# Four edits in a two-block transformer kernel: gate rows under the root, an earlier exponential, output banks closed one by one, and a last norm on two engines

## The chip, the core and the metric

The kernel runs on one core of a Trainium2 chip, alone. The metric is the device time of one execution in microseconds (us), the median of three runs. In the profile the engines are PE (matrix products), PEld (its weight loads), DVE (vector), ACT (scalar), POOL and SP; SP issues nearly all DMAs here. PE has two clock levels, 1.2 and 2.4 GHz; the profile's granted clock is 0.5 at the lower and 1.0 at the higher one.

## What is computed

256 tokens of width 1024 pass through two blocks. The first has two layers (feed-forward, attention, feed-forward, with layer norms). The second has two layers on the same rows, all in fp32:

```python
for i in range(2):
    h = rms_norm(x, norm_g[i, 0]) * (1 + sc1) + sh1
    y = hgrn2_mixer(h, ...) if i == 0 else rglru_mixer(h, ...)   # both end in "@ w_out", 1024 x 1024
    x = x + g1 * y
    h = rms_norm(x, norm_g[i, 1]) * (1 + sc2) + sh2
    x = x + g2 * peer_ffn(h, ...)        # 16384 experts, each head takes its best 16
return rms_norm(x, final_g)
```

In `peer_ffn` each of 8 heads chooses its 16 best experts; their scores go through a softmax (`gate`), and the result is the gated sum of `gelu(h . u) v` over the chosen experts. The attention of the first block ends in a 1024 x 1024 product as well (`mix @ w_out`), followed by a layer norm.

## The kernel before, in words

**Products in split words.** An fp32 product is made of three PE instructions: each operand is split in a rounded high word (ACT writes it) and a rest, the low word (DVE subtracts), and PE adds high x high, high x low and low x high in one PSUM bank. So each tile of weights goes DMA -> ACT (`high`, 128 x 1024) -> DVE (`low`) -> PE. Order on each engine is fixed by its program; engines wait for one another by counting semaphores.

**Expert layer (`peer`, lines 1143, 1732 and 2493).** 272 weight tiles of 512 KB per layer stream through 6 slots. After 16 tiles for the queries come 128 tiles of `u` (the up phase: PE `up(n)`, 24 products of 256 columns in bank n mod 3) and 128 of `v` (the down phase). In the up phase ACT does for each n: wait that PE has finished tile n, GELU of the bank into `arena`, then `high` of tile n + 3 (`early`, line 1753). DVE does `low` of each tile as soon as `high` is there, and between these, the choice of the best 16: comparisons, then at lines 2519 to 2529 the best scores less their maximum are copied to `best` (`best_shifted`), then 12 operations of 128 x 2048 (lines 2541 to 2548) that look up the chosen indices, with 1.5 `low` tiles dealt out after each. Then DVE waits for ACT's exponential of `best` (`best_exp`, line 2552), sums it, inverts, multiplies, signals `choices_ready`, and goes on with `low` tiles. ACT takes the exponential in its loop after `high` of n = BEFORE - 6 = 58:

```python
if n == BEFORE - 6:
    act.wait_ge(S("best_shifted"), l + 1)
    run(best[:, :, :, :], best[:, :, :, :], ACT.Exp).then_inc(S("best_exp"), 1)
```

GELU and the exponential lie in different function tables of ACT, so a table load stands before and after it. PE transposes the choices after n = 61.

**Output products (`out_by_source`, line 1060).** Four such products: `out0` and `out1` (attention, through `mixer_out`), `hg_out` (HGRN recurrence) and `lru_out` (linear recurrence). Eight sources k (128 rows of the weights each) times four PSUM banks Y[n] (two row tiles tt, two halves b, n = 2 tt + b), each k and n a group of three PE instructions of 512 columns, so 96 in all (in `lru_out` the first two k are unsplit). The first six k run source by source over all banks; the last two bank by bank, so that bank 0 is finished first. `out_summed` tells DVE of banks 0 to 2, `piece_done` of the last. Weight pieces hold two k; `piece_done` is also what SP waits for to load the next piece or tile into that slot (lines 458 to 499).

**Norms.** `layer_norm` (lines 1334, 1920) takes for each bank a multiply-add and a statistic on DVE, then aggregates, ACT takes the root (`layer_root`), DVE inverts and normalizes, PE transposes (`turn_rows`), and ACT and DVE write the transposes out (`evacuate`; on ACT the four of tt = 0 stand between its roots of tt = 0 and tt = 1). `rms_norm` (lines 1352, 1969) does `residual` for banks 0 to 2 (two DVE instructions: product with the gate row, sum with x), ACT squares each half with a sum, DVE adds (`rms_total`), ACT takes the root, DVE inverts and scales tt = 0, then comes bank 3. The first use of a root costs ACT a table load.

**Gate rows.** `spread_gates(0)` (line 659) is 16 PE instructions into banks B[0] and B[1]; `take_gate_rows(0)` (line 1393) copies them on ACT. In `hgrn` (lines 996, 1587, 2255) PE makes the means of squares (8 instructions recorded), then waits until ACT has taken all four roots (`hg_o_std` = 4; the first by a square root, the other three by logarithm and exponential, with three table loads), then spreads the gates, then starts `hg_out`; ACT takes the two gate rows before its first source word.

**End of the program (`last_norm`, lines 1377, 2003).** DVE: residual 0, 1, 2, total and inverse of tt = 0, its two output halves (`output(0)`), then residual 3, total and inverse of tt = 1, `output(1)`. SP stores each half of 256 KB when it is written.

## Time and profile before

| what | value |
|---|---|
| median of 3 runs | 3186.16 us (3185.39 to 3187.76) |
| the profiled execution: its own time, its span | 3191.51 us, 3189.3 us |
| mean granted PE clock | 0.985 |
| PE busy / PEld / DVE / ACT / POOL | 96% / 87% / 71% / 49% / 12% of the span |
| 16 DMA engines | 567.89 MB moved, mean 178 GB/s |

The span runs from the first to the last instruction; the run's own time has 2.2 us around it. A busy PE counts its modelled pipelined ends, so 96% is not 96% of the peak. A timeline row gives the start, the duration, the engine, the line of the kernel, the operation with its output and input, and in brackets how long the engine was idle before and who released it. Helpers record most operations: line 352 is every product, line 1310 every ACT instruction, line 2466 the `low` of a tile. `arena` is the large buffer in which `best`, `hg_far` and many others lie; `dense` holds the `high` tiles; `gather` is Y, `turn` is B.

### The profile page before, as it was taken

What the parts mean: (1) busy time and instruction counts of PE and PEld (TensorE: products, weight loads), DVE (VectorE), ACT (ScalarE), POOL (GpSimd) and SP (SyncE); (2) the same over time, 40 slices, a digit from 0 to 9 for tenths busy, and PEclk for the clock granted to TensorE, in tenths of its full rate; (3) what the DMA queues carried; (4) which work ended last, traced back from release to release, by engine and by line L of the source; (5) the groups of instructions that cost most, each with busy time, mean ns of one, the idle gap of its engine ahead of it and who ended that gap; (6) DMA issues with size and microseconds to landing.
All of it is one profiled execution on the core that took longest, in us unless ns stands there. A gap on an engine that the chain in (4) does not pass through costs nothing.

```text
span 3189.3 us, 54293 instructions
## 1 busy us (share of the span) xinstructions
PE 3070.6 (96%) x19644; PEld 2773.3 (87%) x19644; DVE 2262.0 (71%) x3943; ACT 1547.7 (49%) x2637; POOL 373.4 (12%) x228
## 2 busy tenths in 40 slices
PE   8998999999999989899999999999999999999998
PEld 7986898898679978799999988887789999998887
DVE  7756896775575547579889965555578979975555
ACT  5536554654454334454444445454645444444454
POOL 5530563553010000000000000000100000000000
PEclk9999999999999999999999999999999999999999
DMA  8762676875135543145544455555335544445554
GB/s 323 278 247 95 244 277 222 295 289 200 67 119 185 172 144 107 33 161 183 184 133 138 138 172 192 194 193 200 137 125 178 181 141 141 138 164 195 194 191 151
DMA packets 124979, 567.89 MB, mean 178 GB/s; under 512 B 13872, under 2 KB 14000, under 8 KB 97328
## 3 DMA queue, kind: packets, MB, share of 16 engines
q1 hardware_dynamic: 108864, 504.41, 46.0%
q0 software_dynamic: 15264, 58.73, 5.0%
q10 hardware_dynamic: 720, 3.00, 0.2%
q8 instruction: 83, 1.36, 0.2%
q14 instruction: 48, 0.39, 0.0%
HBM read 565.03 MB, written 1.05 MB: 177 GB/s over the span
## 4 chain that ended last, share of the span: by engine, by line
PE 82%; DVE 7%; ACT 3%; issue 1%; DMA 0%; POOL 0%; DVEq 0%; SPq 0%; ACTq 0%
PE turn L352 45%; PE gather L352 36%; DVE ring_low L2033 2%; ACT arena L1310 2%; ACT L1310 1%; PE turn L852 0%; DVE rounded L2044 0%; DVE arena L2444 0%; DVE keyed L1910 0%; DVE arena L1907 0%; DVE x_rows L1966 0%; DVE arena L2303 0%; PE gather L646 0%; DVE arena L1964 0%; DVE arena L2165 0%
## 5 line engine op out<-in xcount | busy, mean ns | idle before, releaser
L1310 ACT ACTIVATE dense<-ring 128x1024 fp32r<-128x1024 f32 x544 | 575.8, 1059 | 385.8 <-PE gather L352 347.1
L2466 DVE TENSOR_TENSOR ring_low<-ring,dense 128x1024 fp32r<-128x1024 f32 x544 | 662.5, 1219 | 75.0 <-ACT dense L1310 73.3
L352 PE MATMUL turn<-expert_src_high,dense 128*128 128x256 f32 x2304 | 667.5, 290 | 12.0 <-DVE ring_low L2466 11.4
L352 PE MATMUL turn<-expert_src_high,ring_low 128*128 128x256 f32 x2304 | 654.8, 284 | 0.0
L352 PE MATMUL turn<-expert_src_low,dense 128*128 128x256 f32 x2304 | 654.8, 284 | 0.0
L352 PE MATMUL gather<-dense 128*128 128x512 f32 x2048 | 631.6, 389 | 2.1 <-DVE ring_low L2466 2.1
L2033 DVE TENSOR_TENSOR ring_low<-ring,rounded 128x1024 fp32r<-128x1024 f32 x264 | 424.9, 1630 | 153.1 <-ACT rounded L1310 153.1
L352 PE MATMUL turn<-rounded 128*128 128x256 f32 x2816 | 513.6, 285 | 16.3 <-DVE ring_low L2033 15.3
L352 PEld LDWEIGHTS turn<-rounded 128*128 128x128 f32 x2816 | 444.3, 193 | 21.8 <-DVE ring_low L2033 17.7
L352 PEld LDWEIGHTS gather<-dense 128*128 128x128 f32 x2048 | 384.4, 188 | 83.0 <-DVE ring_low L2466 2.9
L352 PEld LDWEIGHTS turn<-expert_src_high,dense 128*128 128x128 f32 x2304 | 445.0, 193 | 13.1 <-issue 13.1
L352 PEld LDWEIGHTS turn<-expert_src_low,dense 128*128 128x128 f32 x2304 | 445.3, 193 | 0.0
L352 PEld LDWEIGHTS turn<-expert_src_high,ring_low 128*128 128x128 f32 x2304 | 444.5, 193 | 0.0
L352 PE MATMUL turn<-rounded,ring_low 128*128 128x256 f32 x1408 | 399.9, 284 | 0.0
L352 PE MATMUL gather<-ring_low,dense 128*128 128x512 f32 x1024 | 398.4, 389 | 0.0
L1310 ACT ACTIVATE rounded<-ring 128x1024 fp32r<-128x1024 f32 x264 | 277.3, 1055 | 155.6 <-PE gather L352 83.1
L1310 ACT ACTIVATE arena<-turn 128x512 f32<-128x512 f32 (+13 forms) x362 | 142.2, 394 | 389.6 <-PE turn L352 387.1
L2601 DVE TENSOR_TENSOR dense<-arena,dense 128x256 fp32r<-128x256 f32 x256 | 108.3, 425 | 288.5 <-ACT dense L1310 288.5
L2690 POOL TENSOR_TENSOR arena<-arena 128x1024 f32<-128x1024 f32 x96 | 253.5, 2641 | 179.1 <-ACT arena L1310 122.7
L352 PEld LDWEIGHTS turn<-rounded,ring_low 128*128 128x128 f32 x1408 | 271.8, 193 | 0.0
L1310 ACT ACTIVATE arena<-arena 128x1024 f32<-128x1024 f32 (+4 forms) x257 | 198.7, 796 | 89.7 <-DVE arena L2165 52.1
L352 PE MATMUL gather<-rounded 128*128 128x512 f32 x704 | 225.3, 391 | 7.1 <-DVE ring_low L2033 7.1
(238 smaller groups left out, 3863.3 us busy)
## 6 DMA issues: line engine op xcount, KB each, us to landing
ring<-tiles_in SPq DMA_DIRECT2D x544, 512.0 KB, 3.3
ring<-stream SPq DMA_DIRECT2D x205, 1024.0 KB, 5.0
arena<-ada_in POOLq DMA_DIRECT2D x96, 512.0 KB, 6.0
arena<-tables_in POOLq DMA_DIRECT2D x6, 1024.0 KB, 5.3
arena<-keys_in SPq DMA_DIRECT2D x2, 1024.0 KB, 7.5
arena<-c_in POOLq DMA_DIRECT2D x3, 512.0 KB, 6.4
hT<-x_in SPq DMA_DIRECT2D x1, 1024.0 KB, 4.8
x_rows<-rows_in ACTq DMA_DIRECT2D x1, 1024.0 KB, 17.0
```

Of the source, the lines that this page charges most:

```text
L352: return nc.tensor.matmul(out, lhsT, rhs, start=start, stop=stop, skip_group_check=True)
L1310: return nc.scalar.activation(out, in_, func, **kw)
L2033: V.tensor_tensor(ring_low[:, q % SLOTS, cols].bitcast(R32), ring[:, q % SLOTS, cols], w_high[:, 2 * (i % 2) + b, :], ALU.subtract).then_i ...
L2466: V.tensor_tensor(tile_words(t, ring_low).bitcast(R32), tile_words(t), tile_high[:, t % AHEAD, :], ALU.subtract).then_inc(S("tile_low"), 1)
L2601: V.tensor_tensor(expert_low[:, n % 4, :].bitcast(R32), slots[:, n + 12 * turns, :], expert_high[:, n % 4, :], ALU.subtract).then_inc(S("e ...
L2690: nc.gpsimd.tensor_tensor(ada_prod[:, i % 2, :], ada_w[:, i % 2, :], c_row, ALU.mult)\
```

## The change

- `hgrn`: `spread_gates(0)` no longer waits for the roots; the output product waits, for each bank n, until ACT has read it; ACT takes the gate rows after its second source word and not before its first.
- `peer`: ACT takes the exponential after n = BEFORE - 12 = 52 and not 58, in both layers.
- `out_by_source`: the last `tail` sources run bank by bank, 3 by default (`hg_out`, `lru_out`), 4 for `out0` and `out1`; it was 2. The pieces of the tail are told as done in the last bank.
- `last_norm`: residual 3 stands before the inverse and output of tt = 0; of tt = 1, DVE multiplies half 0 by the gain alone, ACT scales it by the inverse, DVE does half 1, and half 1 of tt = 0 comes last. The order of stores is (0, 0), (1, 0), (1, 1), (0, 1).

```diff
--- before.py
+++ after.py
@@ -507,10 +507,17 @@
                 sp.wait_ge(piece_done, q - SLOTS + 1)
                 load(q, q % SLOTS)
             experts(1)
-            for n in range(4):
-                tt, half = n // 2, slice(n % 2 * 512, (n % 2 + 1) * 512)
-                sp.wait_ge(S("output_ready"), n + 1)
+            def store(tt, b):
+                half = slice(b * 512, (b + 1) * 512)
                 sp.dma_start(out[:, tt, half], out_rows[:, tt, half]).then_inc(S("output_stored"), 16)
+
+            sp.wait_ge(S("output_ready"), 1)
+            store(0, 0)
+            sp.wait_ge(S("output_ready_s"), 1)
+            store(1, 0)
+            for n, tt in ((2, 1), (3, 0)):
+                sp.wait_ge(S("output_ready"), n)
+                store(tt, 1)
             sp.wait_ge(S("output_stored"), 16 * 4)
 
 
@@ -763,7 +770,7 @@
                 def bank_free(n):
                     pe.wait_ge(S("mix_low"), PAIRS * m + n + 5)
 
-                out_by_source(f"out{m}", None, mix_words, ready, bank_free)
+                out_by_source(f"out{m}", None, mix_words, ready, bank_free, tail=4)
 
             def mem_kv(m, first, last):
 
@@ -1053,11 +1060,14 @@
                     last = mm(Y[b4][:, :], mean_mat, hg_far[:, 4 * b4:4 * b4 + 4, :].rearrange("p a t -> p (a t)"),
                               True, True)
                     last.then_inc(S("hg_o_sums"), 1)
-                pe.wait_ge(S("hg_o_std"), 4)
                 spread_gates(0)
-                out_by_source("hg_out", None, expert_src_low, lambda k: pe.wait_ge(S("out_low"), k + 1))
-
-            def out_by_source(name, src, src_low, ready, bank_free=None, native=0):
+
+                def sums_read(n):
+                    pe.wait_ge(*((S("hg_o_std"), 1) if n == 0 else (S("hg_o_log"), n)))
+
+                out_by_source("hg_out", None, expert_src_low, lambda k: pe.wait_ge(S("out_low"), k + 1), sums_read)
+
+            def out_by_source(name, src, src_low, ready, bank_free=None, native=0, tail=3):
 
                 q0 = piece_base(name)
 
@@ -1078,7 +1088,7 @@
                     mm(out, xh, wl, False, False)
                     return mm(out, xl, wh, False, k == KC - 1)
 
-                for k in range(KC - 2):
+                for k in range(KC - tail):
                     weights_ready(k)
                     ready(k)
                     for n in range(4):
@@ -1087,13 +1097,16 @@
                         last = product(k, n)
                     if k % 2 == 1:
                         last.then_inc(piece_done, 1)
-                for k in (KC - 2, KC - 1):
-                    weights_ready(k)
-                    ready(k)
                 for n in range(4):
-                    for k in (KC - 2, KC - 1):
+                    for k in range(KC - tail, KC):
+                        if n == 0:
+                            weights_ready(k)
+                            ready(k)
                         last = product(k, n)
-                    last.then_inc(*((S("out_summed"), 1) if n < 3 else (piece_done, 1)))
+                        if n == 3 and k % 2 == 1:
+                            last.then_inc(piece_done, 1)
+                    if n < 3:
+                        last.then_inc(S("out_summed"), 1)
 
             def lru():
                 q0 = piece_base("lru_in")
@@ -1379,6 +1392,10 @@
                     for b in range(2):
                         rms_square(i, tt, b)
                     take_rms_root(i, tt)
+                act.wait_ge(S("rms_inverse"), TT * (i - LAYER_NORMS) + 2)
+                act.wait_ge(S("out_scaled"), 1)
+                run(out_rows[:, 1, 0:512], n_rows[:, 1, 0:512], ACT.Copy, scale=rms_inverse[:, 1:2])\
+                    .then_inc(S("output_ready_s"), 1)
 
             def source_high(norm, src_high=src_high):
 
@@ -1657,10 +1674,11 @@
                     sl = slice(4 * b4, 4 * b4 + 4)
                     act.wait_ge(S("hg_o_log"), b4)
                     run(hg_std[:, sl, :], hg_std[:, sl, :], ACT.Exp, scale=-0.5).then_inc(S("hg_o_std"), 1)
-                take_gate_rows(0)
                 for k in range(KC):
                     act.wait_ge(S("hg_out_ready"), k + 1)
                     run(expert_src_high[:, k, :].bitcast(R32), hT[:, k, :], ACT.Copy).then_inc(S("out_high"), 1)
+                    if k == 1:
+                        take_gate_rows(0)
 
             def lru():
 
@@ -1812,7 +1830,7 @@
                         early(n, i)
                 for n in range(48, BEFORE):
                     early(n)
-                    if n == BEFORE - 6:
+                    if n == BEFORE - 12:
                         act.wait_ge(S("best_shifted"), l + 1)
                         run(best[:, :, :, :], best[:, :, :, :], ACT.Exp).then_inc(S("best_exp"), 1)
                     if n == BEFORE - 3:
@@ -2002,21 +2020,23 @@
 
             def last_norm(i, r, ready):
 
-                for n in range(4):
+                for n in range(3):
                     residual(r, n, ready)
-                    if n == 2:
-                        rms_total(i, 0)
-                        rms_invert(i, 0)
-                        dve.wait_ge(S("final_loaded"), 16)
-                        output(0)
+                rms_total(i, 0)
+                residual(r, 3, ready)
+                rms_invert(i, 0)
+                dve.wait_ge(S("final_loaded"), 16)
+                output(0, 0)
                 rms_total(i, 1)
+                V.tensor_tensor(n_rows[:, 1, half(0)], x_rows[:, 1, half(0)], final_row[:, half(0)], ALU.mult)\
+                    .then_inc(S("out_scaled"), 1)
                 rms_invert(i, 1)
-                output(1)
-
-            def output(tt):
-                for b in range(2):
-                    V.scalar_tensor_tensor(out_rows[:, tt, half(b)], x_rows[:, tt, half(b)], rms_inverse[:, tt:tt + 1],
-                                           final_row[:, half(b)], ALU.mult, ALU.mult).then_inc(S("output_ready"), 1)
+                output(1, 1)
+                output(0, 1)
+
+            def output(tt, b):
+                V.scalar_tensor_tensor(out_rows[:, tt, half(b)], x_rows[:, tt, half(b)], rms_inverse[:, tt:tt + 1],
+                                       final_row[:, half(b)], ALU.mult, ALU.mult).then_inc(S("output_ready"), 1)
 
             def source_low(stage, src_high=src_high, src_low=src_low):
```

## Rows read from the trace of the kernel before

**Rows 1.** Who waited for whom over the whole span: total us, times, longest us

```profile
DVE arena L2553 <- ACT arena L1310: 18.4, 2, 9.2
```

**Rows 2.** ACT in order of time, first expert layer: start us, us, what, idle before, releaser

```profile
1574.95 1.05 ACT L1310 ACTIVATE dense<-ring 128x1024 fp32r<-128x1024 f32 x1
...
1591.94 0.38 ACT L1310 ACTIVATE arena<-turn 128x256 f32<-128x256 f32 x1 [1.55 <-PE turn L352]
...
1593.29 1.28 ACT L1310 ACT_TABLE_LOAD   x1
1594.58 0.42 ACT L1310 ACTIVATE arena<-arena 128x256 f32<-128x256 f32 x1
...
1602.81 0.39 ACT L1310 ACTIVATE arena<-turn 128x256 f32<-128x256 f32 x1 [6.51 <-PE turn L352]
```

**Rows 3.** DVE in order of time, first expert layer

```profile
1533.73 0.29 DVE L2529 COPY arena<-arena 128x256 f32<-128x256 f32 x1
...
1577.17 2.28 DVE L2544 TENSOR_TENSOR arena<-arena 128x2048 f32<-128x2048 f32 x1
...
1584.67 1.23 DVE L2466 TENSOR_TENSOR ring_low<-ring,dense 128x1024 fp32r<-128x1024 f32 x1 [0.75 <-ACT dense L1310]
...
1596.25 3.49 DVE L2466 TENSOR_TENSOR ring_low<-ring,dense 128x1024 fp32r<-128x1024 f32 x3
```

**Rows 4.** Busy time by windows: PE, PEld, DVE, ACT, POOL, granted clock, DMA, GB/s

```profile
1600.00:1601.00 1.00, 1.00 (x7) 1.00 (x7) 0.00 (x0) 0.00 (x0) 0.00 (x0) 0.50 0.00 0
```

**Rows 5.** ACT in order of time, second expert layer

```profile
2575.25 0.39 ACT L1310 ACTIVATE arena<-turn 128x256 f32<-128x256 f32 x1 [6.79 <-PE turn L352]
```

**Rows 6.** PE in order of time, end of the recurrence

```profile
1319.06 3.70 PE L352 MATMUL gather<-arena,consts 128*128 128x512 f32 x8 [0.78 <-ACT arena L1310]
1328.76 3.78 PE L352 MATMUL turn<-consts,mod 128*128 128x128 f32 x16 [6.00 <-ACT arena L1310]
1334.57 0.47 PE L352 MATMUL gather<-hg_high,expert_src_high 128*128 128x512 f32 x1 [2.03 <-DVE expert_src_low L2357]
```

**Rows 7.** ACT in order of time, end of the recurrence

```profile
1327.04 1.67 ACT L1310 ACTIVATE arena<-arena 128x512 f32<-128x512 f32 x3
...
1333.55 0.42 ACT L1310 ACTIVATE expert_src_high<-hT 128x256 fp32r<-128x256 f32 x1
```

**Rows 8.** Busy time by windows, as in rows 4, gate spread and output product

```profile
1330.00:1331.00 1.00, 1.00 (x6) 1.00 (x6) 0.00 (x0) 0.00 (x0) 0.00 (x0) 0.50 0.00 0
...
1337.00:1338.00 1.00, 1.00 (x4) 0.80 (x3) 0.96 (x3) 0.70 (x2) 0.00 (x0) 0.50 0.00 0
```

**Rows 9.** The chain of work that ended last, between output product and expert layer

```profile
1347.91 5.13 DMA ring<-tiles_in
```

**Rows 10.** DVE in order of time, first row norm after the first output product

```profile
326.82 0.69 DVE L1907 SCALAR_TENSOR_TENSOR arena<-x_rows,gather 128x512 f32<-128x512 f32 x1 [5.50 <-PE gather L352]
```

**Rows 11.** PE in order of time, one of the last products there

```profile
330.62 0.39 PE L352 MATMUL gather<-out_rest,mix_words 128*128 128x512 f32 x1
```

**Rows 12.** ACT in order of time, the same norm

```profile
331.75 1.50 ACT L1310 ACTIVATE hT<-gather,params 128x128 f32<-128x128 f32 x4 [1.53 <-PE gather L646]
...
334.37 0.29 ACT L1310 ACTIVATE keyed<-keyed,consts 128x1 f32<-128x1 f32 x1 [1.12 <-DVE keyed L1915]
```

**Rows 13.** DVE in order of time, after the output product of the linear recurrence

```profile
2326.90 0.69 DVE L1964 TENSOR_TENSOR arena<-gather,arena 128x512 f32<-128x512 f32 x1 [3.41 <-PE gather L352]
```

**Rows 14.** The chain of work that ended last, the same norm

```profile
2331.76 0.30 ACT keyed L1310
```

**Rows 15.** DVE in order of time, the end of the program

```profile
3181.91 0.68 DVE L1964 TENSOR_TENSOR arena<-gather,arena 128x512 f32<-128x512 f32 x1
...
3184.83 1.42 DVE L2018 SCALAR_TENSOR_TENSOR hT<-x_rows,keyed,arena 128x512 f32<-128x512 f32 x2
```

**Rows 16.** Busy time by windows, as in rows 4, the last two stores

```profile
3186.00:3187.00 1.00, 0.00 (x0) 0.00 (x0) 0.25 (x1) 0.00 (x0) 0.00 (x0) 0.50 0.56 209
3187.00:3188.00 1.00, 0.00 (x0) 0.00 (x0) 0.00 (x0) 0.00 (x0) 0.00 (x0) 0.50 0.86 316
```

## The prediction

> **What bounds the kernel now.** PE is busy for nearly all of the span, and the chain of waits runs mostly through it, so time is to be had only where PE stands still or runs at its lower clock. I read first the table of who waited for whom: DVE waited twice, 9.2 us each, at line 2553 for ACT [rows 1]. That is the exponential of the best scores, once per expert layer. Then the three engines in order of time there, then around each output product and at the end, and the granted clock in each of these places.
>
> In the first expert layer ACT takes the GELU of tile 58 at 1591.94 and that of 59 only at 1602.81 [rows 2]. Its pace before is (1591.94 - 1574.67) / 6 = 2.88 us per tile (1574.67 is the GELU of tile 52, 0.28 before the rounding in the rows). DVE, which has the low word of tile 58 done at 1585.9, stands before the exponential until 1595 and can make that of 59 only from 1596.25 [rows 3]. PE has run dry at 1591.92, and starts tile 59 at some 1597.6. The clock has fallen by then, and the tile runs at the lower level [rows 4], 5.2 us instead of 2.9. Together 10.87 - 2.88 = **7.99 us lost**. In the second layer ACT's idle time at the same place is 6.79 instead of 6.51 [rows 2, 5], so 8.27 are lost.
>
> **1. The exponential at tile 52.** ACT has finished rounding tile 55 at 1576.00 [rows 2]. What now follows is load, exponential, load: 1.28 + 0.42 + 1.28 with gaps, 3.01 us, to 1579.03 [rows 2]. Queued behind: the GELU of 53 (before at 1577.55, now 1579.05) and the rounding of tile 56, now done at 1580.4 instead of 1578.9. By the next tile ACT has caught up (it works 1.3 us of each 2.88). Its wait for the shifted scores costs nothing: they are copied at 1533.73 [rows 3], 41 us earlier. DVE's low word of tile 56 then stands from 1580.4 to 1581.6; before it there is the look-up of 2.28 us that ends at 1579.4 [rows 3], behind it one more of that kind, to 1583.8; low word of 57 to 1585.0, of 58 to 1586.1. PE wants these tiles at 1583.3, 1586.2 and 1589.0 (1591.92 less three, two and one times 2.88). The closest slack is 1.2 us. Sum, reciprocal and gates, 1.2 us, follow at once, the low word of 59 waits for its rounding at 1587.5 and is done at 1588.8; PE wants it at 1591.9. So PE doesn't stop. The second layer has the same distances. Gain **7.99 + 8.27 = 16.3 us**. The bounds: nothing, if the tile is held by something that no row shows, and 16.3.
>
> On the table load the Trainium skill (ScalarE: Activation LUTs, section "What ACT_TABLE_LOAD costs") gives about 1.28 us for the load and 1.38 us of drain more, 2.66 us per switch. The trace has 1.28 and the exponential 0.01 us behind it [rows 2], with no drain. By the page ACT would be held 5.8 us and not 3.0, the low word of tile 56 would come at some 1584.3, 1 us after PE wants it, and the sum below would be 2 us smaller.
>
> **2. The gate row spread.** PE ends the means at 1322.76, stands 6.00 us until ACT's last root at 1328.71, spreads the gates in 3.78, and waits 2.03 more until ACT has copied the gate rows and split the first source [rows 6, 7]. Now the spread runs from 1322.8. Its clock is still high there, and at the lower one it took 3.78 [rows 6, 8], so it takes half, to 1324.7, under the roots. ACT goes from its last exponential straight to the first source: 1328.65 instead of 1333.55 [rows 7], 4.9 us earlier, and DVE and PE behind it. The waits per bank are met (the banks are read before ACT's last exponentials). The copies now lie between ACT's second and third source, where ACT stood idle 1.6 us and they take 1.08: nothing. What changes is the clock. Before, the output product had it low around 1337 [rows 8], for 8 instructions of 0.43 instead of 0.23 us, 1.6 us lost, since PE had stood before. Now PE stands from 1324.7 to 1329.7, 5 us; after 5.7 us of standing at the exponential it was low for one tile and cost 2.3. I take 2.0 instead of 1.6. Gain **4.5 us**, bounds 2.5 and 6.5 (the clock not falling at all).
>
> **3. Banks in the tail.** The bounds of the banks' ends follow from the spacing of products: 18 of them lie between the end of bank 0 at 326.80 and that of bank 3 at 331.01 [rows 10, 11], 0.233 each.
> - `out0`, tail 4: bank 0 now ends 18 products earlier (322.6), bank 1 12 (325.4), bank 2 6 (328.2), bank 3 as before. DVE is free (it stood 5.50 us [rows 10]). So tt = 0 is normalized by 328.6, bank 2 taken by 330.0, and bank 3 at 331.05 instead of 332.7. The input of the second root comes at 332.7 instead of 334.35. But ACT's queue has the four write-outs of tt = 0 before it, to 333.25 [rows 12], and these start from PE's transposes, which stay behind the last product. So the root goes from 334.37 to 333.25: **1.1 us**, where DVE alone would give 1.65.
> - `out1` has the same rows 588.5 us later: **1.1 us**.
> - `lru_out`, tail 3: banks 0 to 2 are ready 9, 6 and 3 products earlier, and DVE stood 3.41 us [rows 13]. Bank 1 ends 1.4 us earlier, so ACT's squares and its table load are done at 2330.35; DVE's third residual then ends at 2330.4 and the root comes at 2330.55 instead of 2331.76 [rows 14]: **1.2 us**.
> - `hg_out`, tail 3: DVE and ACT are held there by the first two expert tiles, whose loads wait for the piece of sources 2 and 3 and land 5.13 us later [rows 9]. This piece is finished by product 48 in both kernels: **0**.
>
> Every tail wants source 7 at an earlier product (in `out0` 57 and not 75, 4.2 us earlier); its split is done at 316.7, 5 us before that. The pieces of the tail are told later, so SP loads tiles 2 and 3 of the first expert layer 4.9 us later, at the end of `hg_out`: ready some 6 us before ACT rounds them. Nothing, but were that cover gone, up to 3 us.
>
> **4. The last norm.** Residual 3 starts when bank 3 ends, 3180.57, not at 3181.91 behind the output of tt = 0 [rows 15]. From there to the output took 2.92; half an output (0.71) and a product (0.69) now stand in what was DVE's wait for squares and root (1.5), and stick out by 0.3. So the output starts at 3183.8, ACT and DVE both finish a half by 3184.5, and DVE the last at 3185.2, against 3186.25. The stores are next: 0.56 + 0.86 = 1.42 us of all DMA engines for the last two, 0.71 each [rows 16]. Three now come within 0.8 us. Data had stopped moving 2.3 us after the first of the two was ready (3185.54); now it takes 0.9 + 3 x 0.71 = 3.0 from 3184.5. Gain 3187.85 - 3187.5 = **0.4 us**, bounds -0.5 and 1.1.
>
> **Sum.** 16.3 + 4.5 + 1.1 + 1.1 + 1.2 + 0.4 = 24.6 us. The profiled execution took 3191.51, 5.35 above the median of runs; it becomes 3166.9, and the median 3186.16 - 24.6 = **3161.6 us**, 0.77% less.
>
> **Rivals.**
> - *The exponential's new place starves PE instead.* Closest slack 1.2 us; if tile 56 or 57 comes 2 us late in each layer and the clock falls with it as in [rows 4], 2 x (2 + 2.3) = 8.6 are lost: 3170.2. For it: three engines in a tight sequence; against it: the rows add up, with room. Chance 0.07.
> - *The clock gives more.* PE stands less between the transposes of the two row tiles in `out1` and `lru_out`, and after the spread. If the clock stays high there and in `hg_out`, up to 1.6 to 1.8 us in each of three places: 29.6 less, 3156.6. Chance 0.08.
> - *The exponential is not what holds DVE*, and moving it does nothing to the stop: only 8.3 us remain, 3177.9. Against it: its end at 1595.00 and DVE's next start, 0.1 apart. Chance 0.02.
> - *A table load holds ACT longer than its own row.* Were it more than 1.2 us longer for the pair, the slack is used up and PE stops by the rest: at 2.2 longer 1 us per layer, 3163.6. Against it: the exponential starts 0.01 us after its load [rows 2]. Chance 0.01. (This is what the page's drain would do.)
> - *Slower.* ACT at tile 52 waits for the shifted scores and its rounding queue stands with it. That decides when they come later than 1576.0; PE stops beyond 1577.2, and for a loss of over 6.4 us in all each layer must lose 8.2 + 4.2 + 3.2 = 15.5 us, scores at 1592.7. They come at 1533.73, 59 us before. At 1594.7, 2 us worse still, the kernel takes 3196.6. Chance 0.01; another 0.01 for all else that is slower.
>
> **How the numbers follow.** The forecast has 0.80, its own range by the bounds of parts 2 to 4 is 3158 to 3165; with the two nearest rivals 3157 to 3169.5. About 0.2% (6.4 us) is what a measurement can tell from no change. All cases but the last pass it: faster 0.97, within 0.2% 0.01, slower 0.02.
>
> **What would show it.** Right: no stop of PE between tiles 58 and 59 in either layer, GELUs 2.88 us apart, DVE's wait at line 2553 gone from the table; one longer step at tile 53 on ACT alone. PE's spread directly behind the means and in half the time; `hg_out` starting 1 us after ACT's last exponential. Roots of tt = 1 after `out0` and `out1` right behind four write-outs. Three stores back to back at the end. Wrong: a new PE wait for DVE near tile 56 or 57, an `hg_out` at the low clock for longer than 5 us, a total under 17 us.

## The result, and the profile after

The changed kernel takes 3163.0 us (median of 4 runs, 3161.53 to 3165.44), the kernel before 3186.96 (4 runs, 3185.39 to 3187.84): the ratio is 0.9919 with a 95% interval of [0.9906, 0.9931], 24.0 us less. The forecast was 3161.6. In a later comparison on another chip the changed kernel stood at 3163.9 against 3190.5 (5 and 15 runs, ratio 0.9915 [0.9902, 0.9928]).

| | before | after |
|---|---|---|
| profiled execution, us | 3191.51 | 3161.53 |
| its span, us | 3189.3 | 3159.6 |
| mean granted clock of PE | 0.985 | 0.990 |

So the two profiled executions are 30.0 us apart and the medians 24.0. Of the 30, 5 lie in places that no edit touches, as the comparison of all traces below shows.

**The exponential.** ACT in order of time, first expert layer (start us, us, engine, line, what, idle time before and its releaser); line 1323 is the helper that was 1310:

```profile
1565.19 0.39 ACT L1323 ACTIVATE arena<-turn 128x256 f32<-128x256 f32 x1 [1.55 <-PE turn L352]
1565.47 1.05 ACT L1323 ACTIVATE dense<-ring 128x1024 fp32r<-128x1024 f32 x1
1566.54 1.28 ACT L1323 ACT_TABLE_LOAD   x1
1567.83 0.42 ACT L1323 ACTIVATE arena<-arena 128x256 f32<-128x256 f32 x1
1568.27 1.28 ACT L1323 ACT_TABLE_LOAD   x1
1569.56 0.38 ACT L1323 ACTIVATE arena<-turn 128x256 f32<-128x256 f32 x1
...
1570.95 0.38 ACT L1323 ACTIVATE arena<-turn 128x256 f32<-128x256 f32 x1
...
1573.83 0.39 ACT L1323 ACTIVATE arena<-turn 128x256 f32<-128x256 f32 x1 [1.55 <-PE turn L352]
```

The GELU of tile 52 starts at 1565.19, that of 53 at 1569.56, 4.37 us behind it and so 1.49 late, and that of 54 at 1570.95. At 1573.83 ACT is 2.88 behind again and waits for PE. The exponential starts 0.01 us behind its table load, and the GELU 0.01 behind the second one. DVE in the same stretch:

```profile
1570.92 1.22 DVE L2486 TENSOR_TENSOR ring_low<-ring,dense 128x1024 fp32r<-128x1024 f32 x1 [0.94 <-ACT dense L1323]
...
1574.26 2.35 DVE L2486 TENSOR_TENSOR ring_low<-ring,dense 128x1024 fp32r<-128x1024 f32 x2
1576.53 0.41 DVE L2573 TENSOR_REDUCE arena<-arena 128x16 f32<-128x256 f32 x1
```

The low word of tile 56 comes 5.73 us behind the GELU of tile 52. The reduction that waited for the exponential before (line 2553 there [rows 1], 2573 here) follows at 1576.53 with no wait, and the wait of [rows 1] is gone from the table. The chain of waits has one piece where it had a stop:

```profile
1412.52 178.54 PE turn L352 x1488
```

These are 1488 matmuls without a pause. The piece of before that it answers to ended with tile 58:

```profile
1422.00 169.92 PE turn L352 x1416
```

**The gates.** First the chain of waits at the end of the recurrence (start us, us, what), with `issue` for time in which PE waited for nothing that the profile shows. Then two windows with the granted clock (the third figure from the end, as in [rows 4]):

```profile
1313.31 3.70 PE gather L352 x8
1317.01 1.78 PE turn L352 x16
1318.80 5.02 issue
1323.82 14.10 PE gather L352 x48
```

```profile
1324.00:1325.00 1.00, 1.00 (x3) 0.81 (x4) 0.52 (x3) 0.85 (x3) 0.00 (x0) 0.50 0.00 0
...
1329.00:1330.00 1.00, 1.00 (x4) 0.79 (x3) 0.96 (x3) 0.12 (x1) 0.00 (x0) 0.63 0.00 0
```

The spread is directly behind the sums and takes 1.78 instead of 3.78 us [rows 6]. Then PE stands for 5.02. The output product starts 10.51 us behind the start of the sums, not 15.51, but its first 48 matmuls take 14.10 us and not 12.95: it begins at the lower clock. What comes behind is ACT and DVE with the first two expert tiles:

```profile
1342.62 2.24 ACT L1323 ACTIVATE dense<-ring 128x1024 fp32r<-128x1024 f32 x2 [11.92 <-DMA ring<-tiles_in]
1343.71 2.40 DVE L2486 TENSOR_TENSOR ring_low<-ring,dense 128x1024 fp32r<-128x1024 f32 x2 [12.13 <-ACT dense L1323]
1346.03 0.68 DVE L1982 TENSOR_TENSOR arena<-gather,arena 128x512 f32<-128x512 f32 x1
```

**The tails.** ACT behind `out0`:

```profile
331.94 1.50 ACT L1323 ACTIVATE hT<-gather,params 128x128 f32<-128x128 f32 x4 [4.09 <-PE gather L653]
333.33 0.30 ACT L1323 ACTIVATE keyed<-keyed,consts 128x1 f32<-128x1 f32 x1
```

The second root stands behind four write-outs, as forecast. From the end of the product (331.47, before 331.02) it comes 1.86 us later and not 3.35 [rows 12]. Behind `lru_out` the root comes at 2310.17, 23.12 us behind the start of the product (2287.05), where before it was 25.76 [rows 14].

**The last norm.** DVE, ACT and the stores at the end, and the windows of the last stores (the last two figures are the share of the DMA engines and GB/s, as in [rows 16]):

```profile
3152.87 0.75 DVE L2038 SCALAR_TENSOR_TENSOR hT<-x_rows,keyed,arena 128x512 f32<-128x512 f32 x1
3153.65 2.84 SPq L512 DMA_DIRECT2D out<-hT  x4
3154.42 0.72 ACT L1323 ACTIVATE hT<-arena,keyed 128x512 f32<-128x512 f32 x1 [0.38 <-DVE keyed L1958]
3154.42 1.41 DVE L2038 SCALAR_TENSOR_TENSOR hT<-x_rows,keyed,arena 128x512 f32<-128x512 f32 x2
```

```profile
3156.00:3157.00 1.00, 0.00 (x0) 0.00 (x0) 0.00 (x0) 0.00 (x0) 0.00 (x0) 0.50 1.00 371
3157.00:3158.00 1.00, 0.00 (x0) 0.00 (x0) 0.00 (x0) 0.00 (x0) 0.00 (x0) 0.50 1.07 344
```

Half an output on DVE at 3152.87, half on ACT at 3154.42, the other two on DVE, as forecast. Three stores come close together: the last stores fill two windows where before one had 0.56 and one 0.86.

### The profile page after: what moved, and what is told of

It reads as the page before. It is cut to its first block, busy times and chain, and to the rows that moved or that the text cites. A ratio compares the mean times of both kernels' runs of the same rounds, so it can differ in the third digit from the quotient of the medians.

```text
span 3159.6 us, 54295 instructions
## 1 busy us (share of the span) xinstructions
PE 3057.3 (97%) x19644; PEld 2764.3 (87%) x19644; DVE 2252.5 (71%) x3943; ACT 1547.0 (49%) x2638; POOL 369.4 (12%) x228
## 3 DMA queue, kind: packets, MB, share of 16 engines
q1 hardware_dynamic: 108864, 504.41, 46.4%
HBM read 565.03 MB, written 1.05 MB: 179 GB/s over the span
## 4 chain that ended last, share of the span: by engine, by line
PE 85%; DVE 5%; ACT 3%; issue 1%; POOL 0%; DMA 0%; DVEq 0%; ACTq 0%
PE turn L352 46%; PE gather L352 38%; ACT arena L1323 2%; DVE ring_low L2053 1%; PE turn L859 0%; DVE arena L2464 0%; DVE rounded L2064 0%; ACT L1323 0%; ACT hT L1323 0%; DVE arena L2323 0%; DVE arena L2185 0%; PE gather L653 0%; DVE arena L1963 0%; ACT rounded L1323 0%; DVE arena L2180 0%
## 5 line engine op out<-in xcount | busy, mean ns | idle before, releaser
L2053 DVE TENSOR_TENSOR ring_low<-ring,rounded 128x1024 fp32r<-128x1024 f32 x264 | 416.7, 1596 | 164.5 <-ACT rounded L1323 164.2
```

Source lines behind the costliest of these rows:

```text
L2053: V.tensor_tensor(ring_low[:, q % SLOTS, cols].bitcast(R32), ring[:, q % SLOTS, cols], w_high[:, 2 * (i % 2) + b, :], ALU.subtract).then_i ...
```

## The experiments

Twelve kernels ran, four to a chip, each compared with the kernel before on its own chip. Edits are shown against the kernel named.

| run | runs | median us | before, same chip | ratio, 95% interval |
|---|---|---|---|---|
| exponential alone | 6 | 3180.2 | 3191.3 | 0.9976 [0.9962, 0.9989] |
| gates alone | 12 | 3187.1 | 3191.3 | 0.9986 [0.9969, 1.0002] |
| tails alone | 11 | 3191.5 | 3191.3 | 1.0003 [0.9994, 1.0012] |
| last norm alone | 11 | 3189.6 | 3191.3 | 0.9999 [0.9991, 1.0008] |
| exponential at 57, alone | 12 | 3181.0 | 3189.7 | 0.9974 [0.9965, 0.9983] |
| exponential at 56, alone | 6 | 3174.9 | 3189.7 | 0.9953 [0.9938, 0.9969] |
| after + 44 fillers | 6 | 3165.0 | 3189.7 | 0.9927 [0.9911, 0.9942] |
| after, tiles later | 6 | 3166.5 | 3189.7 | 0.9934 [0.9919, 0.9949] |
| after, exponential undone | 10 | 3184.5 | 3190.5 | 0.9979 [0.9968, 0.9990] |
| after again | 5 | 3163.9 | 3190.5 | 0.9915 [0.9902, 0.9928] |
| after + 20 fillers | 5 | 3165.9 | 3190.5 | 0.9917 [0.9904, 0.9930] |
| after + 20 fillers, tiles later | 6 | 3164.0 | 3190.5 | 0.9920 [0.9903, 0.9937] |

The four parts alone add up to 11.1 + 4.3 - 0.2 + 1.7 = 16.9 us by these medians, not to 24. Parts 2 to 4 together, the run with the exponential undone, stand 6.0 us under before, with an interval that leaves out zero, and alone they add up to 5.8. So what does not add up lies in the exponential.

Single executions of one kernel lie 14 us apart and more (exponential alone: 3175.07 to 3189.16), which is more than most effects sought. So I read the parts from the traces. All kernels issue the same 19,644 matmuls (the fillers come on top), in the same order but for the products that a tail moves within its output product. So the time between two matmuls of the same number can be compared across traces. The stretches below are worked out that way, in us; they are named by the starts in the trace of before: **exp 1** 1590 to 1602.8, **exp 2** 2560 to 2575, **hg** the recurrence's sums to the first expert product (1319.06 to 1367.23), **out0** 326.8 to 346, **out1** 915 to 951.5, **rec 2** 2198 to 2306, **lru** 2306 to 2338.88, **rest** all else from the first matmul to the last, **end** the start of the last matmul to the end of the span.

| trace | exp 1 | exp 2 | hg | out0 | out1 | rec 2 | lru | rest | end |
|---|---|---|---|---|---|---|---|---|---|
| before | 12.79 | 14.97 | 48.17 | 19.19 | 36.40 | 108.02 | 32.88 | 2896.0 | 9.11 |
| after | 4.80 | 6.72 | 44.64 | 18.41 | 35.35 | 106.50 | 29.98 | 2892.6 | 8.65 |
| after again | 4.80 | 6.72 | 44.57 | 17.70 | 34.50 | 106.51 | 29.97 | 2896.4 | 8.65 |
| exponential undone | 12.63 | 14.87 | 44.89 | 16.91 | 34.44 | 107.97 | 33.22 | 2897.8 | 8.64 |
| exponential alone | 4.80 | 6.72 | 46.40 | 20.00 | 36.43 | 108.19 | 32.96 | 2896.3 | 9.12 |
| gates alone | 12.43 | 14.52 | 43.29 | 20.04 | 36.38 | 107.98 | 34.36 | 2896.3 | 9.11 |
| tails alone | 12.43 | 14.84 | 49.00 | 17.68 | 35.39 | 107.99 | 33.08 | 2895.3 | 9.12 |
| last norm alone | 12.44 | 14.51 | 46.38 | 19.22 | 36.41 | 108.00 | 34.38 | 2898.9 | 8.65 |
| at 57 | 9.35 | 11.27 | 45.88 | 20.08 | 36.38 | 107.99 | 34.36 | 2899.7 | 9.10 |
| at 56 | 4.98 | 6.91 | 46.38 | 19.98 | 36.39 | 108.09 | 32.95 | 2900.7 | 9.12 |
| 44 fillers | 4.80 | 6.72 | 44.90 | 16.91 | 34.48 | 107.98 | 29.97 | 2899.3 | 8.64 |
| tiles later | 4.80 | 6.72 | 42.66 | 18.39 | 35.24 | 106.48 | 29.97 | 2898.6 | 8.63 |
| 20 fillers | 4.80 | 6.72 | 40.50 | 17.69 | 34.17 | 109.09 | 31.61 | 2899.5 | 8.66 |
| 20 fillers, tiles later | 4.80 | 6.72 | 40.59 | 18.39 | 35.12 | 108.17 | 31.44 | 2897.5 | 8.66 |

What to see first is the column **rest**. The few edited instructions in it (the exponential's new place, the first products that a tail moves) hold nothing up: 311 to 326.8 of before takes 15.82 and 1570 to 1590 takes 20.04 us in every trace. And yet the column goes from 2892.6 to 2900.7. The profiled execution of after has the lowest of all. The spread lies before 845 of before, in four pieces: up to 280 the traces differ by up to 5.6 us, from 346 to 540 by 4.7, from 540 to 800 by 4.4 and from 800 to 845, in an attention stage, by 6.3. In this last one the lower clock is granted there for about 7 us in the trace of after (and in those of gates alone, tails alone and 20 fillers), 20 in the one with the exponential at 57, and 14 in all others, before among them.

### The exponential alone

```diff
-                    if n == BEFORE - 6:
+                    if n == BEFORE - 12:
```

> The kernel before with the exponential at tile 52 instead of 58, nothing else. Theory: DVE's waits of 9.2 us per layer at the exponential are gone, PE does not stop between tiles 58 and 59, and the run is 16.3 us shorter than the kernel before (15 to 17). Rival, a table load that holds ACT beyond its own row: PE stops by about 1 us in each layer at tile 56 and the gain is 14.3. Rival, PE starved at the new place by 2 us with the clock falling: the gain is 7.7. Rival, the exponential was not the holder: 0.

The trace has what the theory says: 12.79 to 4.80 and 14.97 to 6.72, **16.24 us**. Before's own trace is the longest of the five with the exponential at 58; against the other four it is 15.4 to 16.0. One piece of the chain of waits covers the place:

```profile
1421.54 178.55 PE turn L352 x1488
```

The runs do not: 11.1 us by the medians, 7.6 by the ratio with an interval that ends at 12.1. The profiled execution was 16.4 us under that of before, the fastest of six. Its mean granted clock was 0.988; the other five had 0.982 to 0.986, the slowest of them the lowest, so lower clock elsewhere is where at least part of their time went. That the median gives less than the edited place was the open question, and the run with the exponential undone was made for it.

### The gates alone

```diff
                     last.then_inc(S("hg_o_sums"), 1)
-                pe.wait_ge(S("hg_o_std"), 4)
                 spread_gates(0)
...
-                out_by_source("hg_out", None, expert_src_low, lambda k: pe.wait_ge(S("out_low"), k + 1))
+                out_by_source("hg_out", None, expert_src_low, lambda k: pe.wait_ge(S("out_low"), k + 1), sums_read)
```

Not shown are `sums_read`, the wait per bank, and ACT's gate rows behind its second source word; both are as in the change.

> The kernel before with the gate row spread directly behind the means, nothing else. From the trace of the changed kernel I now expect 3.5 us less: 5.0 us between the sums and the output product, of which 1.5 come back because the product has its first 5.8 us at the lower clock instead of a short piece in the middle. By the sum of the prediction it is 4.5. Rival, the clock stays high when nothing but this is changed: 6.5. Rival, the two expert tiles hold DVE all the same and the start of the product is worth nothing: 0.

By the medians it is 4.3 us, but the interval [0.9969, 1.0002] does not exclude that nothing is gained. In **hg** the trace has 4.9 less than before's own, and 3.1 less than the 46.4 of three other traces with the old order there (exponential alone, last norm alone, at 56). Those differ from before by the clock again: they have no low clock in the product up to its 56th matmul, which the expectations below call tile 49 (12.8 us). Before and this run both have some there (14.4 us each), so 4.9 is the comparison at an equal clock. The start itself is 5.0 us earlier in every trace with the edit (10.51 and not 15.51) but that with 44 fillers.

### The tails alone

```diff
-            def out_by_source(name, src, src_low, ready, bank_free=None, native=0):
+            def out_by_source(name, src, src_low, ready, bank_free=None, native=0, tail=3):
...
-                for k in range(KC - 2):
+                for k in range(KC - tail):
```

> The kernel before with the tails of three and four sources, nothing else (the output product behind the recurrence has its tail too). Theory: 1.1 + 1.1 + 1.2 = 3.4 us less; with what the trace of the changed kernel shows, 1.5 + 1.0 + 1.5 = 4.0, and up to 5.4 if the clock rises earlier in the first expert layer too. Rival, PE waits for the last source, wanted up to 18 products earlier: slower by the wait, 1 us or more. Rival, the later loads of tiles 2 and 3 of the expert layer cost: up to 3 us taken off the gain.

In the runs nothing is gained: 1.0003 [0.9994, 1.0012]. By stretch the gain is 1.5 (**out0**), 1.0 (**out1**), and 1.3 in **lru** against the 34.4 of traces in which the low clock begins at nearly the same place. In **hg** there is a loss, 49.00 to before's 48.17, with the same two stretches of low clock around the start of the product. The loss has its rows, ACT and DVE with the first two expert tiles:

```profile
1350.61 2.24 ACT L1313 ACTIVATE dense<-ring 128x1024 fp32r<-128x1024 f32 x2 [11.46 <-DMA ring<-tiles_in]
1351.71 2.40 DVE L2469 TENSOR_TENSOR ring_low<-ring,dense 128x1024 fp32r<-128x1024 f32 x2 [11.67 <-ACT dense L1313]
```

ACT starts both together, 18.3 us behind the start of the product (1332.30), and DVE ends both low words before its first residual, 21.7 us behind it. In before the loads came one by one, ACT started at 1350.94 and 1353.06, and the residual was 20.7 behind the product's start. What costs is the landing of the second load: both kernels issue it 13.3 us behind the start of the product, but it took 6.15 us here and 5.13 in before [rows 9], and the residual is later by the same 1.0. The loads of tiles 2 and 3, which now come later, are not the cause: in before they are issued at 1353.17 and 1353.54, when the second load has landed (1353.04). Nor does it cost by itself that both are there at once: with the exponential at 57, which has the old tail, they are too, the second load took 4.10, and the residual comes 18.4 us behind the start. Why this load was slow stays open; the last section has what the other traces show of it. So this kernel had 3.8 of gain by stretch and 0.8 given back; the median shows nothing of the 3.0 left. Its interval reaches to 1.9 less, so chance alone would be a rare one, and no stretch of its one trace accounts for the rest: this stays open.

### The last norm alone

```diff
...
+                act.wait_ge(S("out_scaled"), 1)
+                run(out_rows[:, 1, 0:512], n_rows[:, 1, 0:512], ACT.Copy, scale=rms_inverse[:, 1:2])\
+                    .then_inc(S("output_ready_s"), 1)
...
+                rms_total(i, 0)
+                residual(r, 3, ready)
+                rms_invert(i, 0)
...
```

> The kernel before with the new order of the last norm and its stores, nothing else. Theory: 0.4 us less (0.5 from the end of bank 3 to the end of the span, 8.76 to 8.28), which the times can hardly tell from nothing, but the trace can: three stores back to back and the last one's data done 0.3 to 0.5 us sooner after bank 3. Rival, the three stores within 0.8 us hinder each other: 0 to 0.5 us more. Rival, the new piece on ACT comes late and the store of tt = 1's first half ends last: up to 1 us more.

The ratio is 0.9999 [0.9991, 1.0008]: as expected too little for the runs. But **end** is steady: 9.10 to 9.12 in the six traces with the old norm, 8.63 to 8.66 in the eight with the new one, **0.47 us** apart.

### The exponential at tile 57, and at 56

```diff
-                    if n == BEFORE - 6:
+                    if n == BEFORE - 7:
```

> The kernel before with the exponential one tile forward, at 57 instead of 58. Theory (three engines in a row: low word of tile n + 2 behind the exponential): the low word of tile 59 is then done at some 1594.6 where PE wants it at 1591.9, so PE stands 2.7 us instead of 5.7; if its clock stays high that costs 2.7 of the 8.0 per layer, and the gain is 10.6 in all; if the clock falls for the next tile too, 2.3 more are lost per layer and the gain is 6. Rival, the place does not matter until the wait is gone altogether: 0. Rival, any move forward gives the whole 16.

PE's row behind tile 58 in order of time (in brackets the idle time before it), and then the granted clock:

```profile
1597.85 0.35 PE L352 MATMUL turn<-expert_src_high,dense 128*128 128x256 f32 x1 [2.83 <-DVE ring_low L2466]
```

```profile
1597.00:1598.00 1.00, 0.15 (x1) 0.18 (x2) 1.00 (x2) 0.88 (x1) 0.00 (x0) 1.00 0.75 299
1598.00:1599.00 1.00, 1.00 (x6) 1.00 (x7) 1.00 (x2) 0.00 (x0) 0.00 (x0) 0.54 0.00 0
...
1600.00:1601.00 1.00, 1.00 (x7) 1.00 (x7) 0.00 (x0) 0.00 (x0) 0.00 (x0) 0.50 0.00 0
```

PE stood 2.83 us (theory 2.7), and the clock fell behind it for a shorter time than behind the 5.7 us at tile 58: the stretch lost 9.35 - 4.80 = 4.55 and 11.27 - 6.72 = 4.55 us, between the two variants of the theory (2.7 and 5.0). The gain is 3.44 + 3.70 = 7.1; the runs give 8.7. One tile forward takes away not quite half of the loss: the exponential, and behind it the low word of tile 59, comes one step of 2.88 us earlier, and PE had stood 5.7.

With `BEFORE - 8`:

> The kernel before with the exponential two tiles forward, at 56. Theory: the low word of tile 59 is ready at some 1591.7, that is 0.2 us before PE wants it, and the gain is 15 to 16.3, the same as at tile 52: the six tiles are then more than is needed. If the slack is short by up to 1 us, PE stands up to 1 us per layer and the gain is 14. Rival, the slack of six tiles is needed: the gain is under 12.

The stretches take 4.98 and 6.91: 0.2 us are lost in each layer and 15.9 of 16.24 gained; by the medians it is 14.9. Two tiles are nearly enough, six are not needed. That two tiles beat one shows in the runs as well, 3174.9 to 3181.0 on one chip. That six beat one does not: 11.1 and 8.7 us, from different chips, can't be told apart, and there the traces alone decide.

### The fillers

```diff
                 spread_gates(0)
+                for n in range(44):
+                    mm(B[2 + n % 2][:, 0:P], mod[:, 16:17].to_broadcast([P, P]), identity, True, True)
```

> The changed kernel with 44 more products of the gate spread's size between spread and output product, into banks that the product then overwrites: their results are not used, they only keep PE at work while it would stand 5.0 us. Theory (what the changed kernel gives back there is the clock): the product has the high clock from its start, its 48 products to the piece of weights take about 11 instead of 14.1 us, and the run is 1.5 to 2 us shorter than the changed kernel, some 25.5 less than the kernel before. Rival, the two expert tiles hold DVE whatever PE does: at most 0.5 us from the changed kernel. Rival, the extra products run beyond ACT's root and delay the first source: up to 1 us more than the changed kernel.

I had counted 44 products as 44 matmuls; each is two, so they took 9.7 us and held the product up by 4.6. Even so **hg** is 44.90, as in after (44.64): from the start of the product on it took 4.3 less, at the high clock. With 20 of them:

> The changed kernel with 20 filling products instead of 44 behind the gate spread (results not used). In the trace with 44 they ran 4.6 us beyond the point where the first source was there, but the output product then took 12.8 instead of 15.6 us to tile 49 and the rest to the expert layer 17.0 instead of 18.6. Theory: 40 matmuls of 0.11 us fill the 5.0 us in which PE stands, the product starts as in the changed kernel and keeps the high clock, so 4.3 us less than the changed kernel (3 to 4.5). Rival, the clock falls all the same: 0. Rival, the tiles' load holds DVE until the same time: 1 us.

The windows of after at this place are above (0.50 to 1329.7); here:

```profile
1326.00:1327.00 1.00, 1.00 (x11) 1.00 (x11) 0.08 (x1) 1.00 (x3) 0.00 (x0) 1.00 0.00 0
1327.00:1328.00 1.00, 0.89 (x8) 0.70 (x7) 0.07 (x1) 0.89 (x3) 0.00 (x0) 1.00 0.00 0
1328.00:1329.00 1.00, 0.55 (x3) 0.50 (x4) 0.74 (x2) 0.22 (x1) 0.00 (x0) 1.00 0.00 0
1329.00:1330.00 1.00, 1.00 (x6) 0.83 (x5) 0.77 (x2) 1.00 (x3) 0.00 (x0) 1.00 0.00 0
```

PE is busy until 1327.9, the product starts at 1328.45 and the clock stays at its higher level. **hg** is 40.50, **4.1 us less** than after; the piece behind it, 1367.23 to 1400 of before, gives 0.5 of that back (33.2 to 32.6). But the run is no faster than after on the same chip (3165.9 to 3163.9, ratios 0.9917 and 0.9915). In its trace **rec 2** has 109.09 instead of 106.51 and **lru** 31.61 instead of 29.97, 4.2 us back, with two stretches of low clock in places where both traces of after have none. Its **rest** is 3.1 longer than that of after again, too. One trace does not show that the other executions lost it in the same places.

### The expert tiles between the steps of the norm

The edit to after moves ACT's roundings of the first two tiles behind its first square and DVE's low words behind residual 1 and behind the total of tt = 0:

```diff
-                for b in range(2):
-                    rms_square(i, 0, b)
+                rms_square(i, 0, 0)
+                if between is not None:
+                    between()
+                rms_square(i, 0, 1)
```

> The changed kernel, with the rounding of the first two expert tiles on ACT and DVE's low words placed between the steps of the norm instead of before it, in the first expert layer. Theory (behind the recurrence the tiles hold DVE and so the norm, since they wait for a load that the output product's first 48 products release): the first residuals and squares no longer wait for the tiles, and the run is 1 to 1.5 us shorter than the changed kernel. Rival, the tail of the norm is bound by PE's last bank and not by the tiles: 0. Rival, ACT's squares come later behind the roundings: up to 1 us more.

**hg** is 42.66, 2.0 less than after. 0.8 of it is clock (its low stretch began earlier before the product and covers less of it: 14.78 us to the 56th matmul, not 15.57), 1.2 the order of the tiles. In the runs it can't be seen: 0.9934 [0.9919, 0.9949].

> The 20 filling products and the expert tiles placed between the steps of the norm, together, on the changed kernel. In the trace with 44 the first residual started 17.9 us behind the start of the product, held by the low word of the second tile. Theory: at the high clock the first banks end before that, the norm starts with them, and it is 1 to 2 us less than with the 20 alone, 5 to 6 less than the changed kernel. Rival, the last bank ends last and the order of the tiles is worth nothing: the same as with the 20 alone.

**hg** is 40.59, the same as with the fillers alone (40.50), and the median is 3164.0, the same as after (3163.9). The rival holds: with the high clock the last bank ends last and the order of the tiles is worth nothing.

### The exponential undone, and after once more

> The changed kernel with the exponential back at tile 58: the gates, the tails and the last norm without part 1. Theory (the parts add up, and the single runs came out lower than their traces only because executions differ by some us elsewhere, where neither kernel is edited): PE's time from tile 58 to 59 is back at 12.8 and 15.0 us instead of 4.8 and 6.7, and the run is 16.3 us longer than the changed kernel on the same chip, some 8 us under the kernel before. Rival, the parts do not add up and the exponential gives about 8 us, as the ratio of the run with it alone had it: 8 us longer than the changed kernel.

> The changed kernel itself, once more, for comparison with the others of this chip: 24 us less than the kernel before (22 to 26), with single executions up to 4 us apart.

The diff of the first is that of the exponential alone, reversed, on the changed kernel. By medians the exponential is worth 3184.5 - 3163.9 = **20.6 us** here, where alone it gave 11.1. In the trace **exp 1** and **exp 2** differ by 7.83 + 8.15 = 16.0. The rival with 8 us is out. The executions scatter by 3 to 4 us, so 16 is not out by the medians; but the two profiled executions are 21.6 apart too, and what they have beyond 16.0 has a place: **rec 2** and **lru** are 4.7 us longer in the undone kernel (141.19 to 136.48), though all instructions there are the same. The product behind the linear recurrence in the chain of waits, undone and after again, and then the granted clock behind its start in the same order:

```profile
2300.61 24.55 PE gather L352 x79
```

```profile
2289.29 21.56 PE gather L352 x79
```

```profile
2301.00:2302.00 1.00, 1.00 (x2) 0.42 (x2) 0.96 (x3) 0.17 (x1) 0.00 (x0) 0.50 0.06 16
...
2305.00:2306.00 1.00, 1.00 (x3) 0.47 (x2) 1.00 (x3) 1.00 (x3) 0.00 (x0) 0.50 0.00 0
```

```profile
2290.00:2291.00 1.00, 1.00 (x3) 0.38 (x2) 1.00 (x2) 0.49 (x2) 0.00 (x0) 1.00 0.00 0
...
2294.00:2295.00 1.00, 1.00 (x4) 0.43 (x3) 1.00 (x3) 1.00 (x3) 0.00 (x0) 1.00 0.00 0
```

PE stood before this product in both. Undone, the clock is low for its first 6 us; in after it is not low at all. Between the two no instruction differs at this place, only when they get there. This is how a part can be worth 16 at its place and 21 between two executions. For the 11 of the exponential alone it is no explanation: its own trace has 141.15 there, and before 140.90. Where the other five executions ran at the lower clock stays open, since only the profiled one has a trace. In the runs the exponential was worth 11.1, 14.9 (at 56) and 20.6 us on three chips, and 15.4 to 16.2 at its place in the traces.

## Why the prediction was right

The measured 3163.0 is 1.4 us above the forecast and within its range, 3158 to 3165. The mechanism of part 1, two thirds of the sum, is shown; of the others some sizes were off and partly cancelled. Step by step:

- **Part 1, 16.3 us: 16.24 (15.4 to 16.2 by the trace compared with).** The step held in each piece: GELU of 53 late by 1.49 (I said 1.5), low word of tile 56 at 5.73 behind the GELU of 52 (1580.4 - 1574.67 = 5.73), that of 59 done at 1579.28, 14.1 behind (14.13). In all 7 traces with the exponential at 52, exp 1 is 4.80 and exp 2 6.72.
- **The table load.** The Trainium skill (ScalarE: Activation LUTs, "What ACT_TABLE_LOAD costs") has 1.38 us of drain per switch; the trace of after has 0.01 us in its place, behind both loads. ACT's GELU was late by 1.49; by an estimate from the page's drain, twice 1.38 more, it would have been late by some 4.2. The measurement decides against the drain here.
- **Part 2, 4.5 us: 3.5 net.** The start came 5.0 earlier (I had 4.9). The clock was mis-sized: I took a loss of 2.0 us after the edit for one of 1.6 before it. With the fillers as measure, the stop of 5.02 us costs 44.6 - 40.5 = 4.1 of clock, of which 2.8 up to the 56th matmul of the product (15.57 to 12.81). With the gates alone the same stop costs 1.6 up to there (14.42 to 12.8), since less of the low stretch lies over the product, and **hg** gains 4.9. The 2.0 came from the loss behind the exponential, 2.3, where the low clock began while PE still stood and so covered less work; in after nearly all of it lies over the product.
- **`out0` and `out1`, 1.1 each: 1.5 and 1.05.** In after's own trace only 0.8 of the first is left, since the low clock covers more of the work behind it there.
- **`lru_out`, 1.2: 1.2 to 1.5 at the same clock** (34.4 to 33.1 or 33.2; 32.9 to 31.6 or 31.4 where the low stretch is shorter), but 2.9 in after, where the clock did not fall. Part of it goes back at once: the piece behind it, 2338.88 to 2370 of before, takes 31.98 us in after and 31.16 in before, and 30.87 with the tails alone where the traces of gates and norm alone have 30.3, since the low clock behind the norm then covers more work. So 2.1 of the 2.9 are left 30 us later, and 0.7 of the 1.3. That the clock stayed high is the rival "the clock gives more" in one of its three places, with 1.6 us, the price it had, before that piece takes its 0.8.
- **`hg_out`, 0: a loss.** Both kernels finish the piece at product 48, as I said, but I took the time of the load as fixed, 5.13. In the tails-alone trace the second load takes 1.0 longer, and that is the loss. In after ACT starts the first tile at 18.80 from the product's start (1342.62 - 1323.82), where in before it had the second at 18.49 and the first long done, and the residual comes at 22.21 and not 20.73. Of these 1.5 us, 1.15 are the lower clock of the 48 products before the load (14.10 to 12.95) and 0.33 the longer load; they are within the 3.5 of part 2. I had looked for the cost of later loads in tiles 2 and 3.
- **Part 4, 0.4: 0.47.**

The corrected sum for after's own trace is 16.24 + 3.5 + 0.8 + 1.05 + 2.9 + 0.5 = 25.0. That the predicted 24.6 is so near it is in part luck: what the clock and the load took in **hg** and what the clock gave in **lru** nearly cancel. It is luck in part, too, that the medians give 24.0: the same parts measured alone add up to 16.9, and the profiled execution, forecast at 3166.9, took 3161.53. What the profiles differ by beyond it, 30 - 25 = 5 us, is in **rest** (3.4) and **rec 2** (1.5).

## What to carry to other kernels

- Place a table load or another long instruction by how many tiles ahead its neighbours run. Here a move of one tile gave 44% of the gain, a move of two 98%, and the four tiles beyond it only the last 2%.
- A gap of PE that is closed at its start but not at its end can cost a clock phase; price the phase at the place where the work lies that it will cover, not where it covered something else.
- When executions differ by more than the effect, compare the time between the same two matmuls in both traces. It separates a part's own effect (here to some 0.5 us in each stretch) from what the granted clock does elsewhere.

## What was not expected of the hardware

- A stop of 2.83 us of PE (exponential at 57) was followed by the lower clock. But before `lru_out` PE stands 3.11 or 3.12 us in all fourteen traces, and the clock is low behind it in ten and not in four (after, after again, tiles later, 44 fillers). The two executions of the changed kernel agree; what decides it stays open. PE's row there, in before and in after:

```profile
2306.00 8.50 PE L352 MATMUL gather<-ring,arena 128*128 128x512 f32 x16 [3.11 <-DVE arena L2451]
```

```profile
2287.05 7.11 PE L352 MATMUL gather<-ring,arena 128*128 128x512 f32 x16 [3.12 <-DVE arena L2471]
```

- Making PE busy with work that is thrown away saved 4.1 us at its place and nothing measurable in the runs.
- The second of the two 512 KB loads at the end of `hg_out` took 4.06 to 4.98 us in the seven traces whose first 48 products ran at the high clock throughout, and 5.13 to 6.15 in the seven in which part of them ran at the lower one. No run shows why. The first of the two took 3.28 us with the gates alone and 5.28 with the tails alone, issued at the same point of the product and at the same clock.
